# Two-layer attention stage of a float32 block pair: heads taken by pairs on two row tiles, bias added on VectorE, attention weights scaled before they are turned, retention started during the projection

## What is computed

```python
RET_HEADS, RET_DK, RET_DV, FOX_HEADS, FOX_DH, D_FF = 4, 48, 96, 6, 64, 2816

def hybrid_layer(h, ...):
    proj = h @ w_in                                  # q_r k_r v_r g_r u_p q_f k_f v_f f_logit
    o_r = retention_chunkwise(rotary(q_r), rotary(k_r), v_r)   # causal q k^T with decay, no softmax
    o_r = silu(g_r) * head_group_norm(o_r, ret_gn_g)
    o_p = multiscale_pool(u_p, pool_w, pool_scale)
    o_f = forgetting_attention(q_f, k_f, v_f, log_sigmoid(f_logit + b_f))
    h = layer_norm(ALPHA * h + concat(o_r, o_p, o_f) @ w_out)
    return layer_norm(ALPHA * h + (silu(h @ w1) * (h @ w3)) @ w2)

def forgetting_attention(q, k, v, logf):             # per head
    c = cumsum(logf)
    s = (q * d ** -0.5) @ k.T + c[:, None] - c[None, :]
    return softmax(where(causal, s, -1e30)) @ v      # c[:, None] drops out of the softmax
```

## Time and profile before

| what | value |
|---|---|
| median of 3 runs | 3643.5 us (3630.28 to 3646.5) |
| the profiled execution's own time | 3643.83 us |
| its span, first to last instruction | 3641.5 us |
| TensorE matmul busy | 3377.6 us (93%) |
| TensorE weight load busy | 1927.6 us (53%) |
| VectorE busy | 934.8 us (26%) |
| ScalarE busy | 529.6 us (15%) |
| mean granted TensorE clock | 0.940 |

### The profile page before, as it was taken

How to read it: one execution, slowest core, us unless ns; L and a number is a source line. 1 busy time by engine, 2 the same in 40 slices (tenths; PEclk the granted TensorE clock), 3 DMA queues, 4 the chain that set the end, 5 groups by cost and what they waited for, 6 DMA issues and landing times.

```text
span 3641.5 us, 51693 instructions
## 1 busy us (share of the span) xinstructions
PE 3377.6 (93%) x22406; PEld 1927.6 (53%) x22406; DVE 934.8 (26%) x1959; ACT 529.6 (15%) x1107; POOL 45.1 (1%) x58
## 2 busy tenths in 40 slices
PE   8986576889999999999989999999999999999998
PEld 3544365534434443444345467575576747666765
DVE  0235864411221122122260322112122121211101
ACT  0121100011111111111121111031111301021000
POOL 0000000100000000000010000000000000000000
PEclk9975698889999999999999889999999999989999
DMA  9603001489999999999843213133432343233432
GB/s 410 275 0 156 0 1 40 167 340 404 407 414 409 408 409 413 405 406 407 341 161 126 86 47 130 67 139 127 151 116 108 123 158 131 93 116 127 159 153 81
DMA packets 85654, 747.69 MB, mean 205 GB/s; under 512 B 9424, under 2 KB 22144, under 8 KB 45488
## 3 DMA queue, kind: packets, MB, share of 16 engines
q1 hardware_dynamic: 60912, 694.05, 47.9%
q10 hardware_dynamic: 18032, 25.57, 2.1%
q0 software_dynamic: 6608, 26.58, 1.9%
HBM read 679.05 MB, written 67.11 MB: 205 GB/s over the span
## 4 chain that ended last, share of the span: by engine, by line
PE 89%; DVE 6%; DMA 2%; ACT 1%; issue 1%; POOL 1%; ACTq 0%; POOLq 0%; DVEq 0%; SPq 0%
PE psum L996 18%; PE psum L1311 17%; PE psum L1073 9%; PE psum L1328 8%; PE psum L1257 6%; PE psum L659 3%; PE psum L1297 3%; PE psum L651 3%; PE psum L1265 3%; PE psum L667 2%; PE psum L949 2%; PE psum L1226 1%; PE psum L1096 1%; PE psum L1210 1%; PE psum L1212 1%
## 5 line engine op out<-in xcount | busy, mean ns | idle before, releaser
L996 PE MATMUL psum<-weight_ring,arena 128*32 128x512 f32 x6192 | 685.1, 594 | 0.0
L1311 PE MATMUL psum<-arena,weight_ring 128*128 128x256 f32 (+1 forms) x2816 | 645.4, 389 | 2.8 <-ACT arena L1790 2.8
L1311 PEld LDWEIGHTS psum<-arena,weight_ring 128*128 128x128 f32 x2816 | 536.8, 193 | 92.2 <-ACT arena L1790 3.6
L996 PEld LDWEIGHTS psum<-weight_ring,arena 128*32 128x32 f32 x6192 | 195.1, 110 | 419.6 <-issue 407.0
L1073 PE MATMUL psum<-weight_ring,arena 128*32 128x256 f32 x6144 | 338.2, 380 | 1.1
L1328 PE MATMUL psum<-weight_ring 128*128 128x512 f32 x704 | 309.2, 599 | 1.5 <-DVE weight_ring L2592 1.5
L1073 PEld LDWEIGHTS psum<-weight_ring,arena 128*32 128x32 f32 x6144 | 196.8, 110 | 134.6 <-ACT arena L1684 8.6
L651 PE MATMUL psum<-arena 96*128 96x96 f32 (+4 forms) x854 | 124.9, 283 | 117.3 <-DMA arena<-x_sorted 26.6
L2390 DVE COPY arena<-psum 128x384 f32<-128x384 f32 x32 | 17.9, 559 | 814.1 <-PE psum L651 814.1
L1328 PEld LDWEIGHTS psum<-weight_ring 128*128 128x128 f32 x704 | 133.8, 192 | 167.1 <-issue 164.1
L651 PEld LDWEIGHTS psum<-arena 96*128 96x128 f32 (+4 forms) x854 | 93.9, 150 | 218.8 <-issue 151.2
(11 more groups left out here) (392 smaller groups left out, 2898.8 us busy)
## 6 DMA issues: line engine op xcount, KB each, us to landing
weight_ring<-exp_gu SPq DMA_DIRECT2D x129, 2048.0 KB, 12.6
weight_ring<-weights SPq DMA_DIRECT2D x105, 2048.0 KB, 7.8
weight_ring<-exp_down SPq DMA_DIRECT2D x64, 2048.0 KB, 11.7
x_sorted<-arena SPq DMA_DIRECT2D x1, 21504.0 KB, 81.7
arena<-x_sorted ACTq DMA_DIRECT2D x33, 384.0 KB, 10.4
y_sorted<-arena ACTq DMA_DIRECT2D x128, 96.0 KB, 11.9
y_sorted<-arena SPq DMA_DIRECT2D x2, 5632.0 KB, 40.1
y_sorted<-arena SPq DMA_DIRECT2D x2, 5120.0 KB, 44.4
```

The source lines that it names most:

```text
L996: mm = pe.matmul(psum[j * GROUP:(j + 1) * GROUP, g, :], xg[:, k, g * GROUP:(g + 1) * GROUP], w[:, kk, j * 512:(j + 1) * 512], start=(k == ...
L1311: mm = pe.matmul(bank[:, 0:b - a], w[:, k, col:col + P], h2_t[:, k, a:b], start=(k == 0), stop=(k == KT - 1))
```

## The change

- `Plan`: `keys` are now (retention head pair m, key tile), one key tile with both heads a step; `units` are (fox head pair, half of the tiles), 6 in a run, one a step. A's plan has 21 steps (26 before), B's 24 (29 before).
- Scores of two heads go out one after the other, from partitions 0 to 63 and 64 to 127 (`half`), into two different banks. Queries and keys lie in separate arrays (`q_f`, `k_f`, `rot_q`, `rot_k`).
- The bias is no longer accumulated into the scores. Once per head of a pair, at the pair's first unit, it is spread over 128 partitions by a matmul (L1223, L1230), copied to `fox_bias` by ScalarE, and added to the scores of both heads on VectorE (L2605), which writes `fox_p`; mask and maximum now work on `fox_p`.
- After the exponential VectorE takes the reciprocal of the row sums and scales the whole weight rows (L2629), before TensorE turns them.
- The value product has the values as stationary operand (64 columns) and the turned weights as moving one. The two heads write partitions 0 to 63 and 64 to 127 of one bank, so the output is already turned and VectorE copies it to `h2_t` (L2597). `mix` turns only `U_QK`.
- `attend(0, "A")` starts inside `project(0, "A")`, one step ahead of each of its items 7 to 17, and goes on one step ahead of each of items 0 to 9 of `project(0, "B")`. Items 10 to 14 of that projection come after `mix(0, "A")`.
- PSUM: in the fox part `fox_turns` has banks 5 and 6, `fox_outs` has bank 7.

```diff
-        self.keys = [(h, i) for h in range(RH) for i in KEYS[x]]
-        self.pairs = -(-len(self.keys) // 2)
+        self.keys = [(m, i) for m in range(RH // 2) for i in KEYS[x]]
         self.ret_at = len(self.tiles) + 1
-        self.norm_at = self.ret_at + self.pairs + 1
-        self.fox_at = self.norm_at + 1
-        self.units = [(h, u) for h in range(FH) for u in range(2)]
+        self.norm_at = self.ret_at + len(self.keys) + 1
+        self.fox_at = self.norm_at + 2
+        self.units = [(m, u) for m in range(FH // 2) for u in range(2)]
...
+                    if unit is not None and unit % 2 == 0:
+                        pair, extra = score.bank(pe), None
+                        for e in range(2):
+                            h = unit + e
+                            one_row = ident[32:32 + FH, 32 + h:33 + h].broadcast_to([FH, P])
+                            mm = pe.matmul(pair[:, e * BANK:e * BANK + min(b, BANK)], one_row, f_neg[:, 0:min(b, BANK)], start=True, stop=True)
+                        score.ship(mm, ("bias", l, x, unit), "a")
...
+                            for j in range(i + 1):
+                                for e in range(2):
+                                    h = 2 * m + e
+                                    mm = pe.matmul(bank[e * HD:(e + 1) * HD, at:at + SIZE[i]], u2[0:SIZE[j], j, U_VF + h * HD:U_VF + (h + 1) * HD],
+                                                   fox_pt[0:SIZE[j], e, j if i else 4, 0:SIZE[i]], start=(i > 0 and j == 0), stop=(j == i),
+                                                   skip_group_check=True)
...
+                            for e in range(2):
+                                half = slice(e * HD, (e + 1) * HD)
+                                mm = pe.matmul(pair[0:n, e * BANK + c:e * BANK + c + w], q_f[half, m, OFF[i] - a:OFF[i] - a + n], k_f[half, m, 0:w],
+                                               start=True, stop=True, skip_group_check=True)
...
+                            V.did(dve.tensor_tensor(fox_p[0:m, :, c:c + w], both[0:m, :, c:c + w], fox_bias[0:m, :, 0:w], ALU.add),
+                                  score.drained["v"] if i == tiles[-1][0] else None)
...
+                        dve.wait_ge(sem("fox_exp"), len(plan.units) * run + unit + 1)
...
+                            then(dve.reciprocal(row_out[0:m, r:r + 2], row_sum[0:m, r:r + 2]))
+                            for e in range(2):
+                                weights = fox_p[0:m, e, c:c + w]
+                                V.did(dve.tensor_scalar(weights, weights, row_out[0:m, r + e:r + e + 1], None, ALU.mult),
...
-                project(0, "A")
                 steps = attend(0, "A")
-                project(0, "B", steps)
+                project(0, "A", steps, EARLY_STEPS)
+                project(0, "B", steps, range(SPLIT_B), (0, SPLIT_B))
                 each(steps, PLANS["A"].steps)
                 mix(0, "A")
+                project(0, "B", items=(SPLIT_B, 99))
```

More of the change, by code:

```diff
@@ L323, in drained_of, with rest @@
         return self.jobs[self.number[key]]
+    def rest(self, engine):
+        for by, count in self.count.items():
+            if count:
+                engine.wait_ge(self.drained[by], count)
 class BankRing:
@@ L1119, in attend @@
                 a, b = SPAN[x]
[L1120 to L1125, removed]
-                for k in range(plan.steps):
+                for k in range(plan.steps):
+                    if k == 0:
+                        pe.wait_ge(*main.drained_of(("rows", l, x, 1, WHOLE[x][-1])))
+                        if x == "A":
+                            pe.wait_ge(*main.drained_of(("meta", l, x, 1, 0)))
+                        fox_turns.rest(pe)
+                        fox_outs.rest(pe)
                     if 0 <= k - 1 < len(plan.tiles):
@@ L1195, in attend @@
-                        turned[unit] = [turns.ship(mm, ("fox", l, x, unit), "a")]
+                        pe.wait_ge(sem("fox_weights_ready"), len(plan.units) * run + unit + 1)
+                        for e in range(2):
+                            bank = fox_turns.bank(pe)
+                            for i, c in fox_tiles(x, unit):
+                                m, skip = SIZE[i], int(i == 4)
+                                for j in range(skip, i + 1):
+                                    at = c + (j - skip) * m
+                                    mm = transpose(bank[0:SIZE[j], at:at + m], fox_p[0:m, e, c + OFF[j]:c + OFF[j] + SIZE[j]], m)
+                            fox_turns.ship(mm, ("fox", l, x, unit, e), "a")
@@ new lines, in attend @@
+                        score.ship(mm, ("fox", l, x, unit), "v")
+                        if i == 4:
+                            for e in range(2):
+                                bank = fox_turns.bank(pe)
+                                half = slice(e * HD, (e + 1) * HD)
+                                mm = pe.matmul(bank[:, 0:META], q_f[half, m, OFF[i] - a:OFF[i] - a + n], k_f[half, m, BANK:LEN], start=True, stop=True)
+                                fox_turns.ship(mm, ("fox_end", l, x, unit, e), "v")
@@ new lines, in attend @@
+                    t, second = plan.pool_tile(k)
+                    if t is not None and second:
+                        n = SIZE[t]
+                        bank = fox_turns.take(dve, ("pooled", l, t))
+                        for g in range(2):
+                            V.did(dve.tensor_scalar(h2_t[:, 3 + g, OFF[t]:OFF[t] + n], bank[:, g * n:(g + 1) * n], pool_scale[l][:, g:g + 1], None,
+                                                    ALU.mult), fox_turns.drained["v"] if g else None)
@@ L2517, in attend @@
-                    t, second = plan.pool_tile(k)
-                    if t is not None and second:
-                        n = SIZE[t]
-                        bank = turns.take(dve, ("pooled", l, t))
-                        for g in range(2):
-                            V.did(dve.tensor_scalar(h2_t[:, 3 + g, OFF[t]:OFF[t] + n], bank[:, g * n:(g + 1) * n], pool_scale[l][:, g:g + 1], None,
-                                                    ALU.mult), turns.drained["v"] if g else None)
-                    unit = plan.unit(k)
```

427 lines of the change are left out of this document (240 added, 187 removed).

## The result

The changed kernel takes 3528.57 us (median of 4 runs, 3527.24 to 3530.99), the kernel before in the same comparison 3644.95 us (3630.28 to 3646.5). The ratio is 0.969, with a 95% interval of 0.9664 to 0.9716: faster by 116 us, where 81.5 were forecast. The profiled execution took 3528.88 us, its span 3526.8.

The account below looks back on a forecast made before the run. TensorE was taken to bound the kernel, nine tenths of the chain that ended last. From 3643.5 us, -53 - 13 - 2 - 8.5 - 3 - 15 + 8 + 2 + 3 = -81.5 gave 3562 us, range 3535 to 3603.

Parts of the forecast that it names:

- the pairs: Forgetting attention: two heads' products overlap on TensorE, B steps 9.6 us against 15.3, A 6.1 against 9.3; 53 us saved.
- retention: Retention scores: a 256-column pair falls from 1.06 to 0.63 us; 13 us saved over 32 steps.
- Rival 1: Attention pairs overlap less than the first block shows; wholly serial, 32 us are lost, giving 3607 us; chance 0.12.
- I take back 15 of the 25: Half clock in 2016:2143 and 2143:2204: 15 of 25 us lost come back; the ends are 0 and 25.
- +2: Last run's feed_down: 2 us added for the lower clock behind a longer wait, as in 3172:3232.
- pacing: Layer 0: one step an item saves 8.5 of 13.6 us of waits, 5 left for short items; five later items save 3.
- the last run: Last run's feed_down, two steps at a time: waits for the longer chain of 10.9 us against 3.0, so +8 us.
- The output weights: Ahead of two of the four mixes, fewer turns only lengthen TensorE's wait for the output projection's weights; no gain.
- the ring: The two banks of `fox_turns` serve seven jobs in two steps of B: +3 us.
- rival 2: Half clock stays or spreads with denser small products: none of 15 us returns, feed runs lose 10 more; 3587 us, chance 0.12.
- rival 3: VectorE and ScalarE bound every attention unit, making it slower: at 5 us each over 24 units, 3682 us; chance 0.05.
- rival 4: Layer 0's order edit does nothing, waits only move to the early steps: +11.5 us, 3573 us; chance 0.06.

Follow-up runs that it names:

- Experiment 3: Changed kernel with the value product loops swapped, all key tiles of one head before the other head's: 3553.93 us.
- Experiment 1: Changed kernel with layer 0's attention started behind `project(0, "A")` again and two steps instead of one between products of `project(0, "B")`: 3558.90 us.
- experiment 10: Changed kernel with two attention steps instead of one between the products of layer 0's feed_up (0, A): 3549.78 us.
- experiment 2: Changed kernel with the bias accumulated on TensorE in PSUM again, VectorE copying the scores instead of adding: 3545.02 us.
- experiment 9: The kernel of experiment 7 with ScalarE's root of the last tile of feed(0, A) and feed(0, B) moved behind the next mix's copies: 3498.16 us.
- experiment 5: Changed kernel with one step instead of two between the products of the last run's feed_down: 3514.76 us.
- experiment 7: Changed kernel with the edits of experiment 5 and experiment 6 together: 3501.81 us.
- experiment 6: Changed kernel with each piece of the output weights taken at its first product instead of both ahead of the first: 3519.89 us.
- experiment 8: The kernel before the change, unedited, profiled a second time: 3645.98 us, one run.

## Why the prediction was wrong

**Right: the pairs.** Two steps of B take 9.6 us and two of A 5.9, forecast 9.6 and 6.1. They were the largest term, 53 us over six pairs of either kind. Experiment 3 shows the price from the other side: apart, the value products cost 28 us more. In retention a pair of scores of 256 columns takes 0.63 us, as forecast. Rival 1 fell. The share of 3.07 in 4 that the page "TensorE: Matmul & The Clock Gate" of the Trainium skill (Part 3, measured speedup) gives for four row tiles does not carry over to two row tiles here: the two partners' records together take 0.96 us, where one head's took 1.05. Work at full clock fell by 74 us against 68 in the sum. Of the 6 us between, 3 are turns ahead of two output projections, which became wait (below); the rest was not taken apart.

**Wrong: "I take back 15 of the 25".** This term of the clock is the step that failed, in size and in reach. It put 15 us on the two stretches and nothing on the stages behind them. The two stretches of the earlier trace rows gave back all of it: the row for 2016:2089 of the change has the clock at 1.00, and so has 2089:2141.

```profile
2016.00:2089.00 73.00, 71.60 (x348) 41.24 (x346) 25.47 (x76) 33.86 (x98) 0.00 (x0) 1.00 0.26 90
```

And of the stages behind I had costed only 3172:3232, with +2. Whole, they stood at 0.97 and 0.96 over 336 and 389 us, which is 10 and 16 us more; they are now at 0.99 and 0.97. The stage between them went the other way, from 0.99 to 0.98. Over the layers 31 us came back where the sum had 13, and these 18 us are the largest part of the miss. Experiment 1 shows where the first half comes from: with the old place and two steps an item, the clock of stage one is 0.91 again with the new products in it. So most of what I put down to fewer small products was the order. It is not a clean undoing, since a step now holds two heads. The same direction shows in feed_up (experiment 10). The bias products were not the reason (experiment 2).

The same page (section "HAM oscillation") has the clock fall behind waits for a transfer. Its next section, "A second HAM failure mode", has it fall with many short idle times between groups of products. By these two, with the waits gone, the term would have been at most the whole 25 us of the two stretches, 3552 us. The trace agrees in experiments 1, 9 and 10 (0.91 beside 17.9 us of waits, 1.00 beside 4.0, 0.94 beside 25.9), the short waits in 2144:2226 included. It does not in experiment 5, where the two long waits went and the clock stayed at 0.97, nor in the two rows of experiment 7. What lowers the clock stays open beyond this: experiments 1 and 10 add waits and close packing at once, and experiment 7 shows 0.89 and 0.98 with the same order and hardly any wait.

**Nearly right: pacing.** Waits in the first two stages fell from 18.9 to 3.6 us, 15 us against 8.5 + 3 forecast: most of the 5 us that I left for the short items did not arise. The chains are shorter than estimated (5.85 and 4.85 us against 8.2 and 6.8), which fits but was not tested alone. Of the 2.35 us at tile 4, 1.28 are the table load, which I put into the chain because the rows had it there, and 0.5 the scalings. Why the load now stands ahead of ScalarE's wait is not shown: copies stood ahead of the exponential before as well.

**Right with its size off: the last run.** I gave +8 for waits of 10.9 us against 3.0. They are 8.0, so +5; experiment 5 removes them. In layer 0, where I named 3 us for the scaling, there are none. **Right: the output weights.** The DMA wait grew from 1.14 to 7.1 us at one place and from 2.7 to 7.4 at the other. Before, turns of U_G and waits for them stood ahead of it there. From the first turn to the first output product it was 8.0 and 8.2 us before and is 8.0 and 8.2 now, so the edit neither gained nor lost: 3 us of turns became wait. But three things end there within 3 us of each other, and only experiments 6 and 9 together took all of them away. **Not seen: the ring.** +3 us for `fox_turns` shows up as 0.29 us in every other step, about 2 us in all.

**Not of the change: 6.8 us.** The part ahead of the layers differed between the two profiles by that much, and experiment 8 shows the kernel before differing from itself as much. That the time fell below the range, by 6 us, and not just inside it, may be no more than this. Rivals 2, 3 and 4 fell too. For rival 4 it is experiment 1 that says so: the part of the order edit that it undoes, which I had priced at 8.5 us and its share of the clock, is worth 32.7 us in the runs (3558.90 against 3526.21), more than a quarter of the whole gain. The five items behind `mix(0, "A")`, priced at 3 us, were not undone in any run.

## What to carry to other kernels

When a stage's granted clock is below one, cost the half clock for every stage, as 1 less the clock times the length, before costing an edit; where an edit spaces out the small products and takes waits away, the upper end is all of it. Allow some us for scatter too: the same program's first stage had 0.89 and 0.91. Put one step of a dependent chain between two long products, not two: three experiments here (1, 5, 10) price the second step at 7 to 31 us of the layers with not one product more. And behind a wait that the profile names, look for the next one that ends within a few us of it, since removing the named one alone gives only the difference.

## What the runs showed of the hardware

- Two products on two column halves overlap whole, and only as neighbours in TensorE's order: the same value products took 27.4 us interleaved and 55.5 us one head after the other (experiment 3).
- VectorE's scaling by one number per partition, from SBUF, takes 492 ns for 128x528 (L2629), while an add of 128x544 with one operand in PSUM takes 724 ns and a maximum over 128x544 720 ns. The groups of the change, busy us and mean ns:

```profile
L2629 DVE TENSOR_SCALAR weight_ring<-weight_ring,arena 128x528 f32<-128x528 f32 x12 | 5.4, 492 | 0.2
...
L2605 DVE TENSOR_TENSOR weight_ring<-psum,weight_ring 128x544 f32<-128x544 f32 x6 | 4.3, 724 | 7.9 <-PE psum L1273 7.9
L2620 DVE TENSOR_REDUCE arena<-weight_ring 128x2 f32<-128x544 f32 x6 | 4.3, 720 | 0.2
```

- The layers of the change repeat to 0.1 us between two profiles (1605.9 and 1605.9); those of the kernel before differ by 9 us (1713.8 and 1722.8), 8 of it busy time, with 5 us more lost to the half clock.
- The granted clock is not settled by TensorE's order and its waits alone: the same products in the same order had 0.89 beside 1.0 us of waits in one program and 0.98 beside 1.9 us in another (experiments 5 and 7).
